# A transformer's FFN up projection with seven half products in place of eight, on one Trainium2 core: the weight sums made on GpSimd and by adding DMAs

## The reference

```
def conv_ffn(x, w_up, conv_w, conv_b, w_down):    # w_up 1024 x 5632, w_down 2816 x 1024
    h = x @ w_up
    h = causal depthwise convolution of width 3 over the tokens (conv_w) + conv_b
    gate, val = jnp.split(h, 2, axis=-1)
    return (jax.nn.silu(gate) * val) @ w_down
x = x + rms_norm(conv_ffn(rms_norm(x, pre_ffn), ...), post_ffn)
```

## Time and profile before

| what | value |
|---|---|
| median of 3 runs | 2069.28 us (2067.76 to 2073.63) |
| the profiled execution | 2073.53 us, its span 2071.8 us |
| busy share | PE 99%, PE weight load 83%, DVE 68%, ACT 49%, POOL 19% |
| mean granted PE clock | 0.998 of full speed |
| DMA | 251.62 MB, 121 GB/s on average |

### The profile page before, as it was taken

How to read it: one execution, slowest core, us unless ns; L and a number is a source line. 1 busy time by engine, 2 the same in 40 slices (tenths; PEclk the granted TensorE clock), 3 DMA queues, 4 the chain that set the end, 5 groups by cost and what they waited for, 6 DMA issues and landing times.

```text
span 2071.8 us, 32448 instructions
## 1 busy us (share of the span) xinstructions
PE 2053.4 (99%) x11724; PEld 1728.4 (83%) x11724; DVE 1413.2 (68%) x2250; ACT 1023.9 (49%) x1671; POOL 398.3 (19%) x454
## 2 busy tenths in 40 slices
PE   9999999999999999999999999999999999999998
PEld 8889888888988888888877898888878889888886
DVE  5665555999366555699788655456987666554897
ACT  4754333557334433456556644334565764333555
POOL 0520211310000121120045401212200520121220
PEclk9999999999999999999999999999999999999999
DMA  8123322384430332267421113233674131233383
GB/s 287 63 102 102 100 88 95 120 262 157 143 132 31 102 101 92 90 189 244 156 72 42 62 41 104 99 101 96 193 229 163 63 103 60 87 98 101 105 265 117
DMA packets 73881, 251.62 MB, mean 121 GB/s; under 512 B 8448, under 2 KB 12672, under 8 KB 73392
## 3 DMA queue, kind: packets, MB, share of 16 engines
q1 hardware_dynamic: 58752, 213.10, 31.2%
q0 software_dynamic: 7168, 16.78, 3.7%
q10 hardware_dynamic: 7856, 20.34, 2.8%
HBM read 248.04 MB, written 6.34 MB: 123 GB/s over the span
## 4 chain that ended last, share of the span: by engine, by line
PE 85%; DVE 9%; ACT 2%; DMA 2%; issue 1%; POOL 0%; DVEq 0%; ACTq 0%; SPq 0%; POOLq 0%
PE ps L2011 16%; PE ps L2013 16%; PE ps L2012 16%; PE ps L2196 6%; PE ps L2530 4%; PE ps L2532 4%; PE ps L2531 4%; PE ps L2083 2%; DMA raw<-slabs 2%; DVE w_lo L1352 2%; PE ps L2039 2%; PE ps L2041 2%; PE ps L2040 2%; PE ps L2071 1%; PE ps L2055 1%; PE ps L2056 1%
## 5 line engine op out<-in xcount | busy, mean ns | idle before, releaser
L2011 PE MATMUL ps<-h_hi,w_hi 128*128 128x512 f32 (+1 forms) x1552 | 606.6, 391 | 0.0
L2012 PE MATMUL ps<-h_lo,w_hi 128*128 128x512 f32 (+1 forms) x1552 | 603.2, 389 | 0.0
L2013 PE MATMUL ps<-h_hi,w_lo 128*128 128x512 f32 (+1 forms) x1552 | 603.2, 389 | 0.0
L1747 DVE SCALAR_TENSOR_TENSOR work<-ps,conv_sb,work 128x511 f32<-128x511 f32 (+1 forms) x352 | 246.2, 744 | 379.4 <-ACT work L1138 379.2
L1352 DVE TENSOR_TENSOR w_lo<-raw,w_hi 128x1024 fp32r<-128x1024 f32 x356 | 439.1, 1240 | 43.6 <-ACT w_hi L777 39.9
L777 ACT ACTIVATE w_hi<-raw 128x1024 fp32r<-128x1024 f32 x368 | 384.5, 1051 | 129.9 <-DVE raw L1836 71.8
L1138 ACT ACTIVATE work<-ps,conv_sb 128x512 f32<-128x512 f32 x176 | 137.0, 778 | 474.7 <-PE ps L2013 445.5
L2011 PEld LDWEIGHTS ps<-h_hi,w_hi 128*128 128x128 f32 x1552 | 291.4, 188 | 62.6 <-issue 4.0
L2013 PEld LDWEIGHTS ps<-h_hi,w_lo 128*128 128x128 f32 x1552 | 291.3, 188 | 60.5
L2012 PEld LDWEIGHTS ps<-h_lo,w_hi 128*128 128x128 f32 x1552 | 291.5, 188 | 58.6
L718 POOL TENSOR_TENSOR bias<-act 128x256 f32<-128x256 f32 x40 | 78.7, 1967 | 996.4 <-DVE act L1753 996.4
(11 more groups left out here) (289 smaller groups left out, 3367.5 us busy)
## 6 DMA issues: line engine op xcount, KB each, us to landing
raw<-slabs SPq DMA_DIRECT2D x368, 512.0 KB, 3.8
act<-slabs POOLq DMA_DIRECT2D x64, 256.0 KB, 5.5
bias<-slabs SPq DMA_DIRECT2D x16, 512.0 KB, 6.1
act<-slabs SPq DMA_DIRECT2D x12, 512.0 KB, 5.7
bias_dram<-bias_rows ACTq DMA_DIRECT2D x2, 2048.0 KB, 13.3
g_post<-gains ACTq DMA_DIRECT2D x8, 512.0 KB, 4.9
bias<-bias_dram ACTq DMA_DIRECT2D x2, 2048.0 KB, 9.6
g_pre<-gains ACTq DMA_DIRECT2D x7, 512.0 KB, 6.9
```

Source lines behind the costliest of these rows:

```text
L1747: ve.scalar_tensor_tensor(y, ps[:, 2 * par + e, 0:SEQ - sh], conv_sb[:, L, t, tap:tap + 1], y, ALU.mult, ALU.add).then_inc(done, 1)
L2011: pe.matmul(ps[:, bank, cols], hi, h_hi[:, k, cols], start=k == 0, stop=False)
L2012: pe.matmul(ps[:, bank, cols], hi, h_lo[:, k, cols], start=False, stop=False)
L2013: last = pe.matmul(ps[:, bank, cols], lo, h_hi[:, k, cols], start=False, stop=k == KT - 1)
```

## The change

Pairs 4 to 17 of each layer (`FAST` to `FAST_END`) are treated as a 2 x 2 block product. Row 2 is the even (gate) slab, a21 and a22 its two halves of the contraction, row 1 the odd (value) slab, a11 and a12. The input h is cut in two halves of the contraction by two halves of the tokens. Each product then has 4 steps of the contraction by 3 matmuls of 128 x 256, and a pair has seven such products: a11, a12, a22 and the sums x1 = a21 + a22, x2 = x1 + a11, x3 = a11 + a21, x4 = a12 + x2. The gate rows come out with the other sign, which `conv_neg` takes back. POOL adds x1, DVE x2, and two adding DMAs on POOL's queue make x3 (from DRAM) and x4 (from one slot of `raw` to another). ACT copies three partial sums a pair out of PSUM, DVE adds them back (c11, c22, c12). Once a layer DVE joins the parts of h, makes four differences (`join`, `differ`, `in_low`: four operations of 1024 elements each), and ACT makes four high parts (`in_high`); two of the four lie in x's place, so x goes to DRAM and back (4 + 4 DMAs of 512 KB on ACT's queue). The other edits declare semaphores, `conv_neg`, `x_dram` and `x_r`.

```diff
-                ring_slabs(n1 + EARLY, DOWN[L] + FFT)
+                ring_slabs(n1 + EARLY, up_slab(L, FAST + 2))
+                for q in range(FAST, FAST_END):
+                    even = up_slab(L, q + 2)
+                    sp.wait_ge(x4_in[q % 2], sum_count(L, q))
+                    sp.wait_ge(up_lo, 3 * fast(L, q) + 3)
+                    sp.dma_start(raw[:, raw_slot(even), :], slabs[dram(even)]).then_inc(raw_in[raw_slot(even)], 16)
+                    ring(even + 1)
+                ring_slabs(up_slab(L, FAST_END + 2), DOWN[L] + FFT)
...
+                if half == 0:
...
+            def up_sums(L):
...
+                def x1(q):
+                    even = up_slab(L, q)
+                    slot = raw_slot(even)
+                    pool.wait_ge(raw_in[slot], raw_count(even))
+                    pool.tensor_tensor(raw[:, slot, 0:SEQ], raw[:, slot, 0:SEQ], raw[:, slot, SEQ:D], ALU.add).then_inc(x1_made, 1)
+                def x3_x4(q):
+                    even = up_slab(L, q)
+                    row2, row1 = raw_slot(even), raw_slot(even + 1)
+                    pool.wait_ge(up_x2, fast(L, q) + 1)
+                    pool.dma_start(raw[:, row1, 0:SEQ], slabs[dram(even)][:, 0:SEQ], accum_op=ALU.add).then_inc(x3_in[q % 2], 16)
+                    pool.dma_start(raw[:, row1, SEQ:D], raw[:, row2, 0:SEQ], accum_op=ALU.add).then_inc(x4_in[q % 2], 16)
+                x1(FAST)
+                x1(FAST + 1)
+                halves = 0
+                for q in range(FAST, FAST_END):
+                    x3_x4(q)
+                    if q > FAST:
+                        down_sums(L, halves // 2, halves % 2)
+                        halves += 1
+                    if q + 2 < FAST_END:
+                        x1(q + 2)
+                for half in range(halves, 2 * (STEPS - 1)):
+                    down_sums(L, half // 2, half % 2)
...
+                def fast_tap(q, e):
+                    sc.wait_ge(up_c, 3 * fast(L, q) + 2 + e)
...
+                def copy(q, n):
+                    sc.wait_ge(up_mm, 5 * fast(L, q) + (1, 3, 5)[n])
...
+                    sc.activation(kept_sum(q, n), ps[:, up_bank(q, 0), 0:HALF], ACT.Copy).then_inc(up_copy, 1)
...
+                def part_hi(q, name):
...
+                    if name == "x1":
+                        sc.wait_ge(x1_made, fast(L, q) + 1)
+                        sc.wait_ge(w_used, up_slab(L, q - 2) + (1 if q >= FAST + 2 else 2))
...
+                        sc.activation(w_hi[:, s, :], raw[:, row2, :], ACT.Copy).then_inc(up_hi, 1)
...
+                    elif name == "a11":
+                        sc.wait_ge(raw_in[row1], raw_count(even + 1))
...
+                        sc.activation(w_hi[:, 0, :], raw[:, row1, :], ACT.Copy).then_inc(up_hi, 1)
...
+                    elif name == "x3":
+                        sc.wait_ge(x3_in[q % 2], sum_count(L, q))
...
+                        sc.activation(up_parts(q, name)[0], raw[:, row1, 0:SEQ], ACT.Copy).then_inc(hi_made, 1)
+                    else:
+                        sc.wait_ge(x4_in[q % 2], sum_count(L, q))
+                        sc.wait_ge(w_used, up_slab(L, q - 2) + 2)
+                        sc.activation(up_parts(q, name)[0], raw[:, row1, SEQ:D], ACT.Copy).then_inc(hi_made, 1)
...
+                def period(q):
+                    if q > FAST:
+                        copy(q - 1, 2)
+                    copy(q, 0)
+                    if q + 1 < FAST_END:
+                        part_hi(q + 1, "x1")
+                        part_hi(q + 1, "a11")
+                    part_hi(q, "x3")
+                    part_hi(q, "x4")
...
+                    if q > FAST:
+                        fast_tap(q - 1, 0)
+                    copy(q, 1)
+                    if q + 1 < FAST_END:
+                        part_hi(q + 1, "x2")
+                    if q > FAST:
+                        silu((q - 1) % 2, (q - 1) // 2)
+                        fast_tap(q - 1, 1)
...
+                def fast_taps(q, e):
+                    u = UP_SLABS * L + 2 * q + e + 1
+                    for tap, done, earlier, sh in ((1, tap1, tap2, 1), (0, tap0, tap1, 2)):
+                        y = work[:, q % 2, e * SEQ + sh:(e + 1) * SEQ]
+                        scale = conv_sb[:, L, 2 * q + 1, tap:tap + 1] if e else conv_neg[:, L, q - FAST, tap:tap + 1]
+                        ve.wait_ge(earlier, u)
+                        ve.scalar_tensor_tensor(y, ps[:, up_bank(q, e), 0:SEQ - sh], scale, y,
+                                                ALU.mult, ALU.add).then_inc(done, 1)
...
+                def c22(q):
+                    ve.wait_ge(up_copy, 3 * fast(L, q) + 3)
+                    ve.wait_ge(w_used, up_slab(L, q) + 1)
+                    ve.tensor_tensor(ps[:, up_bank(q, 0), HALF:SEQ], ps[:, up_bank(q, 1), HALF:SEQ], kept_sum(q, 2), ALU.add)                      .then_inc(up_c, 1)
...
+                def c12(q):
...
+                    ve.wait_ge(w_used, up_slab(L, q) + 2)
+                    ve.tensor_tensor(o, o, kept_sum(q, 1), ALU.add).then_inc(up_c, 1)
...
+                        ve.wait_ge(hi_made, made(even + (name == "x4")))
+                        ve.tensor_tensor(lo, source, hi.bitcast(f32), ALU.subtract).then_inc(lo_made, 1)
...
+                def x2(q):
...
+                    ve.wait_ge(up_lo, 3 * fast(L, q) + 2)
+                    ve.tensor_tensor(raw[:, row2, 0:SEQ], raw[:, row2, 0:SEQ], raw[:, row1, 0:SEQ], ALU.add).then_inc(up_x2, 1)
...
+                def period(q):
+                    if q > FAST + 1:
+                        fast_taps(q - 2, 1)
+                        gate((q - 2) % 2, (q - 2) // 2)
+                    if q > FAST:
+                        c11(q - 1)
+                    if q + 1 < FAST_END:
+                        part_lo(q + 1, "x1")
+                    if q > FAST:
+                        c22(q - 1)
+                    if q + 1 < FAST_END:
+                        part_lo(q + 1, "a11")
+                        x2(q + 1)
+                    part_lo(q, "x3")
+                    part_lo(q, "x4")
...
+                    if q > FAST:
+                        fast_taps(q - 1, 0)
+                    if q + 1 < FAST_END:
+                        part_lo(q + 1, "x2")
+                    if q > FAST:
+                        c12(q - 1)
...
+                def product(q, e, half, name, operand, begin, onto=False):
+                    o = ps[:, up_bank(q, e), HALF * half:HALF * (half + 1)]
+                    (hi, lo), (b_hi, b_lo) = up_parts(q, name), operand
+                    for k in range(KT // 2):
+                        w = slice(k * P, (k + 1) * P)
+                        pe.matmul(o, hi[:, w], b_hi[:, k, :], start=begin and k == 0, stop=False, skip_group_check=onto)
+                        pe.matmul(o, hi[:, w], b_lo[:, k, :], start=False, stop=False, skip_group_check=onto)
+                        last = pe.matmul(o, lo[:, w], b_hi[:, k, :], start=False, stop=k == KT // 2 - 1, skip_group_check=onto)
+                    return last
...
+                def p1_p2(q):
...
+                    pe.wait_ge(up_lo, 3 * fast(L, q) + 2)
+                    product(q, 0, 0, "a11", h_quarter(0, 0), True).then_inc(up_mm, 1)
+                    product(q, 1, 0, "a12", h_quarter(1, 0), True).then_inc(up_mm, 1)
...
+                def p4(q):
+                    pe.wait_ge(up_copy, 3 * fast(L, q) + 3)
...
+                    product(q, 0, 0, "a22", in_parts(3), False, True).then_inc(w_used, 1)
...
+                def p6_p5(q):
+                    pe.wait_ge(up_copy, 3 * fast(L, q) + 1)
+                    pe.wait_ge(up_lo, 3 * fast(L, q) + 3)
...
+                    product(q, 0, 0, "x2", in_parts(2), False, True).then_inc(up_mm, 1)
+                    product(q, 1, 1, "x1", in_parts(0), True).then_inc(up_mm, 1)
...
+                def p3(q):
+                    pe.wait_ge(up_c, 3 * fast(L, q) + 2)
+                    pe.wait_ge(lo_made, made(up_slab(L, q, 1)))
+                    product(q, 1, 1, "x4", h_quarter(1, 1), False, True).then_inc(w_used, 1)
+                def p7(q):
+                    pe.wait_ge(up_copy, 3 * fast(L, q) + 2)
+                    pe.wait_ge(lo_made, made(up_slab(L, q)))
+                    product(q, 0, 0, "x3", in_parts(1), False, True).then_inc(up_mm, 1)
...
+                for q in range(FAST, FAST_END):
+                    p1_p2(q)
+                    if q > FAST:
+                        p4(q - 1)
+                    p6_p5(q)
+                    if q > FAST:
+                        p3(q - 1)
+                    p7(q)
```

More of the change, by code:

```diff
@@ L34 @@
 UP_SLABS = 2 * FFT
+FAST, FAST_END = 4, 18
 STEPS = FFT // 2
@@ L1152, in pair @@
                     split_hi(n0 + 2 * c + 1 + AHEAD, i)
+                for t in range(TT):
+                    sc.wait_ge(xn_made, TT * (2 * L + 1) + t + 1)
+                    sc.dma_start(x_dram[t], x[:, t, :]).then_inc(x_out, 16)
                 end = FFT // 2 - 1
```

(77 more changed lines are left out.)

162 lines of the change are left out of this document (156 added, 6 removed).

## The result

| | kernel before | changed kernel |
|---|---|---|
| median of the runs | 2071.45 us (2067.76 to 2076.08, 4 runs) | 2220.15 us (2217.11 to 2224.19, 4 runs) |
| span of the profiled execution | 2071.8 | 2220.4 |
| busy share PE, DVE, ACT, POOL | 99%, 68%, 49%, 19% | 93%, 79%, 53%, 26% |

The ratio is 1.0718 (1.0687 to 1.0749). I forecast 2106 us and a range of 2066 to 2150. The sign was right, the size was not, and the time lies outside the range.

A forecast was written before the change was run, and what follows sets the result against it. PE bounded the kernel at 10.88 us a pair; an 11.07 us three-engine round plus 0.33 for POOL gave 11.40, so 29 us over 56 pairs plus 8 for the layers, on 2069.3: 2106 us, range 2066 to 2150.

The forecast's parts named there:

- What PE saves: PE in the fast pairs: 84 matmuls at 0.12 us take 10.08 us, 0.80 us a pair under the former 10.88.
- The longest round: From p4 over ACT's x1 high and DVE's chain to p7 and the next p4: 11.07 us a pair.
- POOL beside DVE: POOL's additions and DVE's SBUF operations hold each other up in each fast pair: 0.33 us, bringing it to 11.40.
- Rival 3, POOL's turns: POOL's x1 holds the SBUF ports for its whole length, delaying a11 low: pair 12.36 us, 2160 us in all; 10%.
- low parts of 1024 elements that last 2 us and more: Sign in DVE's 1024-element low parts that POOL's turns on the ports decided: they would last 2 us and more.
- a pair above 12.3 us: Sign in the fast pairs' length: above 12.3 us means a wait that the prediction did not see.
- Rival 2, the DMA round: Round over x4's adding DMA and the next slab sets the pace: 12.05 us a pair, 2142 us; 16%.
- Rival 1, PE's pace: In the fast pairs PE never waits before p7 and keeps the pace: 10.08 us a pair, 2032 us; 15%.
- The 4 MB of x: nothing: Moving x to DRAM and back each layer costs nothing, as DMA is a third busy there.
- A wait or two: Filling and emptying the new order at PE, with POOL's late sums: 2 us a layer, 8 us in all.

The follow-up runs named there:

- e5: Changed kernel with both POOL's x1 additions and its down-projection half sums cut to 16 columns: 2142.8 us, ratio 1.0336.
- e9: Changed kernel with ten matmuls whose results nobody reads put in where PE waits before p7: 2206.9 us, ratio 1.0659.
- e4: Changed kernel with x4 added by POOL itself in place of an adding DMA: 2341.3 us, ratio 1.1308.
- e1: Changed kernel without x4's adding DMA and the waits for it: 2279.8 us, ratio 1.1012.
- e3: Changed kernel with x4's adding DMA issued before x3's: 2216.9 us, ratio 1.0708.
- e10: Changed kernel with x1 and the half sums on POOL cut to 16 columns and x4's adding DMA left out: 2148.5 us, ratio 1.0378.
- e7: Changed kernel with POOL's half sums held back until DVE's c12 of the pair before: 2215.8 us, ratio 1.0688.
- e8: Changed kernel with half sums held until c12, x4's DMA before x3's, and x3 and x4 parts before the next x1 on ACT and DVE: 2419.4 us.
- e11: As e10, with x3's parts made before the next pair's x1 and a11 parts on ACT and DVE: 2127.9 us, ratio 1.0278.

## Why the prediction was right in sign and wrong in size

- **What PE saves** was right: 0.12 us a matmul, and PE had time left over in every pair.
- **The longest round** was named rightly, link by link, and came to 11.34 us for 11.07, 0.27 too little. In e5's pair at 311.68 half of that lies between p7's start and x1 high (6.09 us for 5.95), the other half from x1 low to p7 (4.17 for 4.04). PE's wait before p7 in e5 is 0.85 us, forecast about 1. Over 56 pairs the clean loss is 26 us where this step alone would have given 56 x 0.19 = 11.
- **POOL beside DVE is the step that failed.** I had 0.33 us a pair, from a rate of 0.40 and the share of the round in which DVE has no slack. The term measures (2220.15 - 2142.8) / 56 = 1.38. The rate was right: over all 56 pairs DVE's four operations lose 1.17 us a pair to 2.95 us of additions, 0.40, which is the 1.18 that I called "all of it". (In the stretch from 240 to 380 us of layer 0 alone it is 1.46, or 0.50.) The share was wrong: all of it counts, not 4 of 11 us. With either kind of addition alone the kernel loses just what DVE loses, 0.34 and 0.48 us a pair. My own working was off besides, as 1.18 x 4 / 11 is 0.43 and not 0.33. I spread POOL's work evenly over the round, but its place is fixed by the waits. x1 begins when its slab lands, and in layer 0 it stops x2 four times, the low part of x3 four times and that of x4 twice. x2 then releases the DMA issues and, 1.15 us behind the first, the sums, which stop the low parts of x4 and x2, never that of x3. In the order of the program all four stand ahead of p7 or of c12 and the copy, where PE waits. I had these waits in the program and did not use them for this term.
- **The clock was no term of my sum at all.** In the pair shown PE's 1.8 us of idle time were followed by some 3 us at the lower level (granted clock 0.63 from 304.4 to 309.0), 1.40 us lost, while after 0.85 us idle in e5's pair the starts stay 0.12 us apart. It happens 19 times in 56 pairs, and not after every such wait. Taken away (e9) it is worth only 13 us, since the branch over c12 and the copy is nearly as long.
- **Rival 3, POOL's turns,** was nearest for the pair: I priced it at 12.36 us and gave it 10%. In the pair shown x1 low to p7 is 0.95 us longer for 1.29 forecast, and POOL stops DVE at x2, one operation behind where I had put it; in other pairs it is a later one. The sign that I gave for this rival, low parts of 1024 elements that last 2 us and more, did not come: they last 1.23 us in the mean. The sign of a wait that I had not seen, a pair above 12.3 us, did. The Trainium skill ("SBUF — State Buffer", Who interferes with whom) has the instruction issued first keep the ports to its end. The x2 of the timelines fits: POOL's x1 starts at 301.06, gets on when a11 low ends at 301.99 and ends at 303.12, and x2 ends 0.55 us later. The 4.25 us of e4 don't fit a single turn: there DVE stands behind four of POOL's instructions, as POOL stood behind several of DVE's in the 6.47 us of the earlier trace rows. I had used those as evidence against turns; they were evidence for something worse.
- **Rival 2, the DMA round,** fell as long as the order is the changed kernel's (e1, e3, e10), although my 4.75 us for x4 was too low (6.6 in the median). It decides as soon as something holds POOL's queue (e7, e8).
- **Rival 1, PE's pace,** fell: in the clean version PE waits before p7, 8.5 us in ten waits of 240 to 380 us.
- **"The 4 MB of x: nothing"** was wrong. I read the mean DMA share (0.30 to 0.36 in the earlier trace rows) and not what stands behind the burst: four loads of 512 KB at once make one slab late, and DVE, full there as I had read in the same rows, has nothing to put into the wait. 10 us.
- **"A wait or two" for filling and emptying**, 2 us a layer with the loss of POOL's late sums, was a guess with no row behind it. It is 9 us without the burst, most of it waits of PE at both ends and the clock that they cost.

No version ran faster than the kernel before. e11, with two costs cut away that the change can't do without, still stands 58 us above it, since the round of DVE and ACT that is left is as long as a pair of before.

## What to carry to other kernels

Work that is put on POOL beside a DVE full of two-operand SBUF operations is not free, and its price is set by which DVE operations it meets: find the wait that releases it and read what DVE does at that moment, and don't spread it evenly. If that operation stands in the round that sets the pace, count the whole of what DVE loses. When PE loses its place as the bound, its waits may cost twice, once as idle time and once as a lower clock afterwards. A mean DMA share says nothing of a burst: look at which transfer queues behind it, and who waits for that.
